# Output projection of a hybrid encoder layer: eight written-out passes, another split of the bank emptying, and the last group's tail rearranged

## The reference, cut to what matters

```
out = jnp.concatenate([attn, y_ssm], axis=-1) @ w_out      # (tokens, 2048) @ (2048, 2048)
y = x + gate * _rmsnorm(out, g_post)                       # gate: one row of 2048 per sequence
```

## Time and profile before

| | |
|---|---|
| runs, median (lowest, highest) | 2302.9 us (2300.42, 2304.52) |
| the profiled execution's own time | 2313.74 us |
| its span, first to last instruction | 2311.9 us |
| mean granted TensorE clock | 0.950 |
| PE, DVE, ACT, POOL busy | 92%, 54%, 31%, 13% |
| `project_out`, first w_out matmul to the end | 1835.6 to 2311.9 us |

### The profile page before, as it was taken

The page is one execution under the profiler, slowest core; times in us unless marked ns, Lnnn a source line. Parts: engine busy times, 40 slices in busy tenths (PEclk is TensorE's granted clock), DMA queues, the critical chain, the costliest instruction groups (busy, mean ns, idle before and its releaser), DMA issues. The chain is left out here.

```text
span 2311.9 us, 33438 instructions
## 1 busy us (share of the span) xinstructions
PE 2137.5 (92%) x12705; PEld 1886.4 (82%) x12705; DVE 1253.8 (54%) x2489; ACT 719.3 (31%) x1407; POOL 311.2 (13%) x588
## 2 busy tenths in 40 slices
PE   6898898999999999999999997799898899998996
PEld 4578887888899999999999996678786678875784
DVE  5455645444423888887777663667663352123224
ACT  5331122111133333333332211545453242221331
POOL 0254343455400000000000000000000200004001
PEclk9899899999999999999999998899998599999997
DMA  9863356655543333333333433734421222227335
GB/s 350 319 172 88 113 131 143 169 175 170 155 111 81 91 91 96 87 95 97 92 104 95 100 91 123 193 109 144 110 87 45 80 73 74 77 78 218 97 94 178
DMA packets 375899, 288.66 MB, mean 125 GB/s; under 512 B 124809, under 2 KB 317521, under 8 KB 374457
## 3 DMA queue, kind: packets, MB, share of 16 engines
q1 hardware_dynamic: 350050, 249.62, 39.4%
q10 hardware_dynamic: 24368, 33.18, 4.3%
q0 software_dynamic: 1328, 3.80, 0.5%
HBM read 226.32 MB, written 60.20 MB: 124 GB/s over the span
## 5 line engine op out<-in xcount | busy, mean ns | idle before, releaser
L1293 PE MATMUL ps_z<-h_hi,w_hi 128*128 128x384 f32 (+2 forms) x1936 | 666.7, 344 | 0.0
L1295 PE MATMUL ps_z<-h_hi,w_lo 128*128 128x384 f32 (+2 forms) x1936 | 657.1, 339 | 0.0
L1294 PE MATMUL ps_z<-h_lo,w_hi 128*128 128x384 f32 (+2 forms) x1936 | 656.9, 339 | 0.0
L1293 PEld LDWEIGHTS ps_z<-h_hi,w_hi 128*128 128x128 f32 (+1 forms) x1936 | 363.4, 188 | 15.9 <-issue 5.6
L1294 PEld LDWEIGHTS ps_z<-h_lo,w_hi 128*128 128x128 f32 (+1 forms) x1936 | 363.4, 188 | 5.0
L1295 PEld LDWEIGHTS ps_z<-h_hi,w_lo 128*128 128x128 f32 (+1 forms) x1936 | 362.9, 187 | 5.3
L877 DVE TENSOR_TENSOR w_lo<-w_raw,w_hi 128x512 fp32r<-128x512 f32 (+1 forms) x172 | 123.2, 717 | 354.7 <-ACT w_hi L543 353.1
L2663 DVE TENSOR_TENSOR o_lo<-o_raw,o_hi 128x512 fp32r<-128x512 f32 x128 | 90.3, 706 | 283.8 <-ACT o_hi L2619 283.7
L543 ACT ACTIVATE w_hi<-w_raw 128x512 fp32r<-128x512 f32 (+1 forms) x172 | 107.5, 627 | 259.7 <-DMA w_raw<-in_w_in 200.6
L2619 ACT ACTIVATE o_hi<-o_raw 128x512 fp32r<-128x512 f32 x128 | 81.1, 634 | 312.1 <-PE ps_out L2804 241.1
L1009 DVE MAX8 top<-score 128x8 f32<-128x1024 f32 (+5 forms) x192 | 171.1, 891 | 3.4
(11 more groups left out here) (436 smaller groups left out, 3169.0 us busy)
## 6 DMA issues: line engine op xcount, KB each, us to landing
w_raw<-in_w_in SPq DMA_DIRECT2D x176, 256.0 KB, 3.1
wada<-in_w_ada SPq DMA_DIRECT2D x32, 1024.0 KB, 9.1
o_raw<-in_w_out SPq DMA_DIRECT2D x128, 256.0 KB, 3.0
wg<-in_w_ada SPq DMA_DIRECT2D x32, 512.0 KB, 4.9
zt<-z_sb ACTq DMA_DIRECT2D x28, 576.0 KB, 4.3
g_raw<-in_w_glu SPq DMA_DIRECT2D x24, 512.0 KB, 4.3
xs<-in_x_prompt SPq DMA_DIRECT2D x8, 1024.0 KB, 6.9
iq_raw<-zt SPq DMA_DIRECT2D x48, 128.0 KB, 3.3
```

The source lines that it names most:

```text
L1293: M(to, w_hi[q][:, k, 0:m], h_hi[:, kk, cols], start=kk == 0, stop=False)
L1294: M(to, w_hi[q][:, k, 0:m], h_lo[:, kk, cols], start=False, stop=False)
L1295: return M(to, w_lo[q][:, k, 0:m], h_hi[:, kk, cols], start=False, stop=kk == KB - 1)
```

## The change

- All eight passes are written out; no loop at run time is left.
- A bank is emptied by two engines: ACT squares it (`out_rows` now takes the squares in float32, and is overwritten), then DVE copies it into `out_rows`. PE waits for DVE's copy alone.
- The gate is multiplied in one pass later: in passes 2 to 8 PE spreads the gate for each tile of the pass before (after pieces 2, 4, 6, ...), and DVE multiplies (`times_gate`) at pieces 3, 5, 7, .... For pass 8 itself the gates are spread at pieces 9 to 12 and ACT keeps them in SBUF (`last_gate`, in the place of `attn_lo`), and DVE's emptying multiplies instead of copying.
- Group 0 is finished over passes 5 to 8, five quarter tiles in each: one DVE instruction (`add_x`) multiplies by 1/rms and adds x. SP loads 256 KB of x and stores 256 KB for each.
- Group 1 is finished after pass 8 by sixteen `add_x`, with nothing on POOL or PE. Its x is loaded as whole rows, four loads of 1 MB, at pieces 9, 11, 13 and 15 of pass 8, over `attn_hi`. SP and ACT store quarter tiles in turn (22 DMAs each).
- `rstd(0)` moves into pass 5: its first half after piece 1, the square root on ACT after piece 2, the rest after piece 3.

```diff
-            def send(g, c, kb):
-                for f in finals_at(g, c, kb - 2):
-                    if f >= 2:
-                        sp.wait_ge(y_ok[f % 2], f // 2)
-                    load_x(sp, 0, f)
-                for H in half_at(g, c, kb - 4):
-                    store_half(sp, 0, H)
...
+            for n, (g, q) in enumerate(PASSES):
                 for kb in range(KB):
+                    m = KB * n + kb
+                    if m >= 2:
+                        sp.wait_ge(w_lo_ok, m - 1)
+                    sp.dma_start(w_raw[:, m % 2], wv[:, kb, cols(q)]).then_inc(w_in[m % 2], 16)
...
+                    if n == NOC - 1 and kb in (4, 6):
+                        load_x(sp, (kb - 4) // 2)
+                    if kb >= 1 and early_at(n, kb - 1) is not None and early_at(n, kb - 1) + 2 < len(early):
+                        f = early_at(n, kb - 1)
+                        sp.wait_ge(y_ok, f + 1)
+                        load_x(sp, f + 2)
+                    if kb >= 2 and early_at(n, kb - 2) is not None:
+                        f = early_at(n, kb - 2)
+                        sp.wait_ge(y_ok, f + 1)
+                        store(sp, 0, *early[f])
+                    if n == 2 * NOC - 1 and kb in (9, 11, 13, 15):
+                        i = (kb - 9) // 2
+                        sp.wait_ge(w_used, used(KB * n + 2 * i + 1))
+                        for p0, rows_n, v in pieces(GROUP_TILES[1][0] + i, *xv):
+                            sp.dma_start(x_rows[i][p0:p0 + rows_n, :], v).then_inc(x_rows_in[i], 16)
+            for f in range(0, len(late), 2):
+                sp.wait_ge(y_ok, len(early) + f + 1)
+                store(sp, 1, *late[f])
...
ACT, end of a pass:
+                for i in range(width(n)):
+                    act.wait_ge(out_mm, done(n, i))
+                    A(rows[i][:, cols(q)], ps_o[i][:], ACT.Square, accum_out=ssq[:, i, q:q + 1]).then_inc(squared, 1)
...
DVE:
+            def evict(n, i):
+                part = rows[i][:, cols(PASSES[n][1])]
+                dve.wait_ge(squared, done(n, i))
+                if n == LAST:
+                    dve.wait_ge(gate_kept, i + 1)
+                    V.tensor_tensor(part, ps_o[i][:], last_gate[:, i], ALU.mult).then_inc(gated, 1)
+                else:
+                    V.tensor_copy(part, ps_o[i][:]).then_inc(evicted, 1)
+
+            def times_gate(n, i):
+                part = rows[i][:, cols(PASSES[n][1])]
+                dve.wait_ge(g_mm, done(n, i))
+                dve.wait_ge(evicted, done(n, i))
+                V.tensor_tensor(part, part, ps_g[(done(n, i) - 1) % 2][:], ALU.mult).then_inc(gated, 1)
+
+            def add_x(i, q, x):
+                part = rows[i][:, cols(q)]
+                V.scalar_tensor_tensor(part, part, stat[:, 4, i:i + 1], x, ALU.mult, ALU.add).then_inc(y_ok, 1)
...
+                    if gate_at(n, kb) is not None:
+                        times_gate(n - 1, gate_at(n, kb))
+                    f = early_at(n, kb)
+                    if f is not None:
+                        dve.wait_ge(gated, done(early[f][1], early[f][0]))
+                        dve.wait_ge(x_in[f % 2], x_landed(f))
+                        add_x(*early[f], xs[:, f % 2])
+                if n + 1 < len(PASSES):
+                    low(KB * (n + 1))
+                for i in range(width(n)):
+                    evict(n, i)
...
PE:
+                    for i in range(width(n)):
+                        if n and kb == 0:
+                            pe.wait_ge(evicted, done(n - 1, i))
...
+                    if gate_at(n, kb + 1) is not None:
+                        spread_gate(n - 1, gate_at(n, kb + 1))
+                    if n == LAST and 0 <= kb - KEEP_AT < TILES1:
+                        spread_gate(n, kb - KEEP_AT)
```

More of the change, by code:

```diff
@@ L2457, in project_out @@
         yv = (out["y_prompt"].rearrange("b t d -> (b t) d"), out["y_sample"].rearrange("b t d -> (b t) d"))
[L2459 to L2465, removed]
+        PASSES = [(g, q) for g in range(2) for q in range(NOC)]
         HALF_D = D_MODEL // 2
@@ L2514, in tiles_before, with cols @@
[L2514 to L2532, removed]
+        def cols(q):
+            return slice(OC * q, OC * q + OC)
@@ new lines, in project_out, with gate_at, early_at @@
+        early = [(i, q) for q in range(NOC) for i in range(TILES0)]
+        late = [(i, q) for i in range(TILES1) for q in range(NOC)]
+        LAST = len(PASSES) - 1
+        KEEP_AT = 9
+        def gate_at(n, kb):
+            i = (kb - 3) // 2
+            return i if n and kb >= 3 and kb % 2 and i < width(n - 1) else None
+        def early_at(n, kb):
+            if PASSES[n][0] == 0:
+                return None
+            first = 4 if PASSES[n][1] == 0 else 2
+            i = (kb - first) // 2
+            if kb < first or (kb - first) % 2 or i >= TILES0:
+                return None
+            return TILES0 * PASSES[n][1] + i
@@ new lines, in y_stored, with x_landed, load_x, store @@
+        def y_stored(q, g):
+            return sum(16 * len(pieces(t0 + i, *yv)) for t0, n in GROUP_TILES[:g + 1] for i in range(n))
+        def x_landed(f):
+            return sum(16 * len(pieces(GROUP_TILES[0][0] + early[h][0], *xv)) for h in range(f % 2, f + 1, 2))
+        def load_x(eng, f):
+            i, q = early[f]
+            for p0, m, v in pieces(GROUP_TILES[0][0] + i, *xv):
+                eng.dma_start(xs[p0:p0 + m, f % 2], v[:, cols(q)]).then_inc(x_in[f % 2], 16)
+        def store(eng, g, i, q):
+            for p0, m, v in pieces(GROUP_TILES[g][0] + i, *yv):
+                eng.dma_start(v[:, cols(q)], rows[i][p0:p0 + m, cols(q)]).then_inc(y_out[q], 16)
@@ L2564, in _ @@
[L2564 to L2573, removed]
+                    sp.dma_start(post[32 * q:32 * q + COND, :], io["g_post"][:, half].broadcast_to([COND, HALF_D])).then_inc(rows_in, 16)
@@ L2610, in _ @@
             A = nc.scalar.activation
[L2612 to L2619, removed]
@@ L2622, in body, with root @@
+            def root(g):
+                act.wait_ge(rstd_step, 8 * g + 2)
+                A(stat[:, 2], stat[:, 1], ACT.Sqrt).then_inc(root_ok, 1)
+            mix_high(0)
+            high(0)
+            for n, (g, q) in enumerate(PASSES):
                 for kb in range(1, KB):
-                    if first_chunk(g, c):
+                    if n == 0:
                         mix_high(kb)
[L2625 to L2630, removed]
@@ L2657, in _ @@
+                for i in range(width(n)):
+                    act.wait_ge(out_mm, done(n, i))
+                    A(rows[i][:, cols(q)], ps_o[i][:], ACT.Square, accum_out=ssq[:, i, q:q + 1]).then_inc(squared, 1)
+            root(1)
+            for f in range(1, len(late), 2):
+                act.wait_ge(y_ok, len(early) + f + 1)
+                store(act, 1, *late[f])
         @block.vector
```

260 lines of the change are left out of this document (104 added, 156 removed).

## The result

| | before | after |
|---|---|---|
| median (lowest to highest), us | 2302.18 (2300.42 to 2304.52) | 2287.82 (2285.08 to 2288.66) |
| ratio, 95% interval | | 0.994, 0.9927 to 0.9953 |
| span of the profiled execution | 2311.9 | 2285.2 |

Faster by 14.4 us, half of the 28.8 forecast. The spans differ by 26.7, and 12 of that lie ahead of `project_out`: its first w_out matmul is at 1835.6 in the profiled execution of before and at 1823.7 after (all other traces of this study have it between 1817 and 1827). From that matmul to the end it is 476.3 us before and 461.5 after, 14.8 less, which agrees with the medians. So the prediction was right to carry a difference over to the median, and all that follows is read in `project_out`.

What follows compares the result with a forecast made beforehand. TensorE was taken to bound most passes, SP's program with late w_out loads pass 5. Terms 5.3 - 30.3 + 3.0 + 4.6 - 11.4 = -28.8 from 2302.9 gave 2274.1 us; own range 2266 to 2281, eight in ten 2261 to 2289.

Steps and rivals of the forecast that it cites:

- I take 1 us a pass: Passes 5 to 7: late loads of w_out behind the early steps cost 1 us a pass, bounds 0 and 5 x 2.1.
- I take 3 us: Pass 8: stalls from four 1 MB loads of x joining the w_out loads cost 3 us, bounds 0 and 12.
- The rival of a crowded pass 8: Pass 8: large x loads crowd w_out, stalls of 12 us instead of 3, whole kernel 2283; chance 0.17.
- The gates: Passes 2 to 8: each of 36 single gate matmuls costs PE 0.53 us, between 0.23 and 0.87.
- the pair's 0.87: Pass 5 before the change: two neighbouring gates cost PE 0.87 us, including some 0.11 of slower spacing afterwards.
- The rival of nearly free gates: Passes 2 to 8: gates at 0.23 save 10.8 us, absent stalls 6 more, whole kernel 2257; chance 0.10.
- The boundaries: Ends of passes: with emptying split between ACT and DVE, each boundary costs 0.2 us, bounds 0 and 1.5.
- `times_gate` hidden: DVE's gate multiplication delays the next `low` by 0.7 us, hidden in 1.3 spare; otherwise 0.7 for each of 32 gates.
- The tail: After the last matmul: 20.0 us against 31.4, a change of -11.4, bounds 19 and 24; last add ends at 14.7.
- three limits together: Tail: adds give 19.6 us, store bytes at 324 GB/s give 20.2, issuing 22 DMAs a queue gives 20.0.
- Early steps as dear as the pairs: Passes 5 to 8: 20 steps at 2.05 us cost 41 instead of 4, whole kernel 2311, slower; chance 0.05.

Runs made afterwards that it cites:

- Experiment 1: The changed kernel, but SP loads x for an early step one piece later, behind the next load of w_out: 2275.86 us, ratio 0.9886.
- experiment 2: The changed kernel, but the four 1 MB loads of x for group 1 all come after the last load of w_out: 2284.35 us, ratio 0.9927.
- experiment 10: The kernel of experiment 7 with all of group 1's x loaded behind the last load of w_out: 2261.95 us, ratio 0.9825.
- experiment 8: The kernel of experiment 1 with group 1's x as eight halves of 512 KB at pieces 5 to 12 of pass 8: 2274.48 us, ratio 0.9878.
- experiment 6: The changed kernel with the gate products over all 128 partitions instead of 64, which gives another y: 2279.23 us, ratio 0.9905.
- experiment 5: The changed kernel with the old emptying in passes 1 to 7, ACT squaring and copying, DVE copying nothing: 2290.54 us, ratio 0.9953.
- experiment 3: The changed kernel, but PE spreads each gate one piece earlier than DVE's `times_gate` needs it: 2290.42 us, ratio 0.9956.
- experiments 6 and 7: The second of these: experiment 1 plus gate products over 128 partitions, with zeros in a second `sel` keeping y right: 2268.60 us, ratio 0.9852.
- experiment 4: The changed kernel, but the tail stores two quarter tiles together, 11 DMAs on each queue instead of 22: 2290.13 us, ratio 0.9937.

## Why the prediction was half right

In `project_out`, so as the sum was made:

| term | forecast | measured | after, forecast | after, measured |
|---|---|---|---|---|
| pass 1 | 0 | -0.4 | 63.7 | 63.3 |
| passes 2 to 4 | +5.3 | +6.5 | 171.8 | 173.0 |
| pass 5 | -30.3 | -28.1 | 47.4 | 49.7 |
| passes 6 and 7 | +3.0 | +6.5 | 93.8 | 97.2 |
| pass 8 | +4.6 | +10.4 | 50.7 | 56.5 |
| tail | -11.4 | -9.6 | 20.0 | 21.8 |
| sum | -28.8 | -14.8 | | |

(Terms are taken from times to 0.01 us and rounded.) Every sign that was forecast is right, but every cost except pass 1's was set too low and every gain too high; 14 us in all. 2287.8 us lies outside the forecast's own range of 2266 to 2281, though inside its eight in ten.

- *The failed step: "I take 1 us a pass"* for late loads of w_out, in the part on finishing group 0. The chain was described as the timeline shows it (wait for `add_x`, three issues, a load 2.1 to 2.8 late), but its slack was worked out with a landing of 3.0 from a trace in which no x lay ahead. It was 3.8 in the median and 4.35 in the step shown, so 2.8 late plus 0.8 to 1.3 stood against 2.8 of slack. Experiment 1 puts 7.8 us on it in passes 5 to 7, 2.6 a pass and not 1: inside the bounds of 0 and 10.5, but nearly three times the term. The steps in pass 8, of which three still load x, were given nothing in the sum, although they come in the same order; there it cost 4.0 more.
- *"I take 3 us" in pass 8.* Without stalls, and with gates as measured, it would be 43.5 + 8 x 0.62 = 48.5; it was 56.5, so 8 us of stalls for 3. It is the term that missed by most. The order alone takes 4.0 of them away (experiment 1), the late loading of x alone 5.8 (experiment 2), so the two overlap; with both gone, and cheap gates, almost nothing is left (experiment 10). The rival of a crowded pass 8 had the second mechanism. Its price was 9 us over the forecast's term, and the stalls are 5 over it, partly by the order; it reckoned with 225 GB/s from the earlier trace rows, and 270 moved at a full share in experiment 8.
- *The gates*: 0.53 was taken. Pass 2 is 54.4 and five gates, and experiment 6 leaves 0.1 for the boundary, so (57.6 - 54.4 - 0.1) / 5 = 0.62 each; 36 x 0.09 are 3.2 us more of work for TensorE. The slower spacing around the gate was in the pair's 0.87; wrong was to take 0.34 off it for the second gate, which cost 0.25. Most of a gate's price is the step between 64 and 128 partitions, which the prediction had no word for. The 216 ns that the prediction quotes from the Trainium skill, "TensorE: Matmul & The Clock Gate", section "Back-to-back issue gap", stand there as the gap of isolated matmuls, beside 131 ns for a stream; the places here are 0.2267 us, and no row shows 131. The rival of nearly free gates was false for this kernel; it came true only once the operands filled all partitions.
- *The boundaries*: 0.2 taken, about 0.1 found; experiment 5 confirms where the gain is from.
- *`times_gate` hidden*: right (experiment 3).
- *The tail*: the start and the sixteen adds came as forecast (14.0 to the last add for 14.7). Of "three limits together" it was the pace of the stores, 262 GB/s and not the 324 taken from a stretch of before that mixed loads and stores: 4.19 MB / 262 = 16.0 instead of 12.9, 3.1 more, of which 1.8 appeared. Why they moved at 262 stays open.
- *Early steps as dear as the pairs*: false. The fifteen steps of passes 5 to 7 cost (146.9 - 139.1) / 15 = 0.52 us each; slower than before would have taken 1.64.
- *Slips in the working*: a boundary was taken at 0.2, but the sums of passes 5 to 7 have 0.3 and that of pass 8 none; and the rival of the early steps counts 4 us of them in the sum, where it holds 3. They make less than 1.5 us together.

## What to carry to other kernels

On a queue that streams operands, issue the stream's next load ahead of any wait for another consumer: a wait and three issues in front of it, which made it some 2 us late in each of eighteen steps, cost 12 us here, and moving a few lines gave that back. When loads are added to a stream, work out its slack with the landing time under the new traffic, and count the bytes of each stretch. Where one wait ends last, little else that is gained shows: the cheap gates and the split emptying brought their time almost only in the passes where w_out was not late.

## What the runs showed of the hardware

A 512-column matmul over 64 partitions between ones over 128 costs 0.62 us of the stream, one over all 128 with zeros 0.23 (experiments 6 and 7); a second one over 64 partitions right behind the first added only 0.25.

At a nearly full share the DMA engines moved very different amounts. In the tail of the changed kernel stores in rows of 2 KB moved 262 GB/s at a share of 0.87, in experiment 4 stores in rows of 4 KB 236 at 0.90. The tail of the tenth kernel has the same 44 stores in rows of 2 KB, but they queue up behind the late loads of x:

```profile
2240.00:2244.00 4.00, 0.00 (x0) 0.00 (x0) 3.59 (x6) 0.00 (x0) 0.00 (x0) 0.50 1.02 231
...
2248.00:2252.00 4.00, 0.00 (x0) 0.00 (x0) 2.81 (x5) 0.00 (x0) 0.00 (x0) 0.50 1.06 397
2252.00:2256.00 4.00, 0.00 (x0) 0.00 (x0) 0.00 (x0) 0.00 (x0) 0.00 (x0) 0.50 1.06 399
```

```profile
2249.03 2.74 DVE L2721 SCALAR_TENSOR_TENSOR out_rows<-out_rows,out_stat,x_rows 128x512 f32<-128x512 f32 x4 [0.96 <-DMA x_rows<-in_x_sample]
```

The last x has landed when DVE's wait for it ends at 2249.03. So in the first stretch loads of x and stores overlap, at 231 GB/s; from 2249.03 on there are stores alone, at 399. The same stores, issued one by one as the adds end, went at 262. A share near 1 is therefore no sign that the engines move all they can, and "the bytes bind" can't be read from it. Whether the deeper queue makes the difference no run here shows.
